# Rows of 276 instead of 272 values for the split activations of a two-block transformer kernel

## What is computed

```python
mod = silu(c) @ ada_w + ada_b            # six shifts, scales and gates
h = modulate(rmsnorm(x, norm1_g), shift1, scale1)
proj = h @ w_in                          # queries, keys, values of two attentions, two gates
merged = sigmoid(ga) * (swa(...) @ w_branch_a) + sigmoid(gb) * (moba(...) @ w_branch_b)
x = x + gate1 * (merged @ w_out)
h2 = modulate(rmsnorm(x, norm2_g), shift2, scale2)
x = x + gate2 * (square(relu(h2 @ w_mlp_in)) @ w_mlp_out)      # 1024 -> 4096 -> 1024
```

```python
h = h + 0.5 * swiglu(rmsnorm(h), w_gate, w_up, w_down)         # 1024 -> 2816 -> 1024
h = h + pool_mixer(...)      or   h + mla_attention(...)       # layer 0, layer 1
h = h + 0.5 * swiglu(...)
```

## Time and profile before

| what | us |
|---|---|
| median of 3 runs | 1241.94 |
| the three runs | 1241.94, 1241.97, 1241.2 |
| span of the profiled execution, first to last instruction | 1239.2 |
| PE busy | 1215.1 (98%) |
| PE weight loads busy | 1192.2 (96%) |
| DVE busy | 862.2 (70%) |
| ACT busy | 634.1 (51%) |
| POOL busy | 174.9 (14%) |

### The profile page before, as it was taken

How to read it: one execution, slowest core, us unless ns; L and a number is a source line. 1 busy time by engine, 2 the same in 40 slices (tenths; PEclk the granted TensorE clock), 3 DMA queues, 4 the chain that set the end, 5 groups by cost and what they waited for, 6 DMA issues and landing times.

```text
span 1239.2 us, 23766 instructions
## 1 busy us (share of the span) xinstructions
PE 1215.1 (98%) x9956; PEld 1192.2 (96%) x9956; DVE 862.2 (70%) x1214; ACT 634.1 (51%) x985; POOL 174.9 (14%) x178
## 2 busy tenths in 40 slices
PE   6999999999999999999999999999999999999997
PEld 4999999999999999999999999999999988999996
DVE  6789888776656766556766665767666777766653
ACT  6557546674445444434544454445454567554531
POOL 3025333000322000012100001310001221000021
PEclk9999999999999999999999999999999999999999
DMA  9987774667564555654455555455555533655641
GB/s 356 326 338 263 245 255 165 233 247 246 166 217 151 181 171 172 202 175 132 134 173 173 180 192 185 148 184 184 199 176 186 188 119 107 205 182 191 198 140 35
DMA packets 67563, 239.17 MB, mean 193 GB/s; under 512 B 7380, under 2 KB 9573, under 8 KB 67456
## 3 DMA queue, kind: packets, MB, share of 16 engines
q1 hardware_dynamic: 66800, 235.41, 56.5%
q0 software_dynamic: 656, 2.24, 0.5%
HBM read 236.55 MB, written 1.07 MB: 192 GB/s over the span
## 4 chain that ended last, share of the span: by engine, by line
PE 93%; DVE 2%; issue 0%; ACT 0%; POOL 0%
PE G L610 28%; PE G L609 28%; PE G L611 28%; PE A L609 1%; PE A L611 1%; PE A L610 1%; DVE sb_wlo L1567 0%; PE A L761 0%; PE A L1055 0%; PE A L776 0%; PE A L749 0%; PE G L1110 0%; PE G L1112 0%; PE G L1111 0%; PE A L1089 0%; PE A L639 0%
## 5 line engine op out<-in xcount | busy, mean ns | idle before, releaser
L1567 DVE TENSOR_TENSOR sb_wlo<-sb_raw,sb_whi 128x1024 fp32r<-128x1024 f32 (+1 forms) x398 | 488.1, 1259 | 81.0 <-ACT sb_whi L1168 80.7
L609 PE MATMUL G<-sb_xh,sb_whi 128*128 128x256 f32 (+2 forms) x1752 | 496.4, 283 | 0.4 <-DVE sb_wlo L1567 0.4
L1168 ACT ACTIVATE sb_whi<-sb_raw 128x1024 fp32r<-128x1024 f32 (+1 forms) x397 | 404.6, 1044 | 180.1 <-PE G L611 161.4
L610 PE MATMUL G<-sb_xl,sb_whi 128*128 128x256 f32 (+2 forms) x1752 | 496.7, 283 | 0.0
L611 PE MATMUL G<-sb_xh,sb_wlo 128*128 128x256 f32 (+2 forms) x1752 | 495.1, 283 | 0.0
L609 PEld LDWEIGHTS G<-sb_xh,sb_whi 128*128 128x128 f32 x1752 | 329.7, 188 | 0.9 <-DVE sb_wlo L1567 0.7
L611 PEld LDWEIGHTS G<-sb_xh,sb_wlo 128*128 128x128 f32 x1752 | 329.4, 188 | 0.0
L610 PEld LDWEIGHTS G<-sb_xl,sb_whi 128*128 128x128 f32 x1752 | 329.2, 188 | 0.0
L609 PE MATMUL G<-sb_hh,sb_whi 128*128 128x256 f32 (+1 forms) x1056 | 297.4, 282 | 1.3 <-DVE sb_hh L1808 1.3
L611 PE MATMUL G<-sb_hh,sb_wlo 128*128 128x256 f32 (+1 forms) x1056 | 297.8, 282 | 0.0
L610 PE MATMUL G<-sb_hl,sb_whi 128*128 128x256 f32 (+1 forms) x992 | 280.8, 283 | 0.0
(11 more groups left out here) (335 smaller groups left out, 1226.7 us busy)
## 6 DMA issues: line engine op xcount, KB each, us to landing
sb_raw<-in_wstream SPq DMA_DIRECT2D x438, 512.0 KB, 4.4
sb_raw<-in_wstream SPq DMA_DIRECT2D x8, 320.0 KB, 7.2
sb_bias<-bias_scratch POOLq DMA_DIRECT2D x1, 2048.0 KB, 16.9
sb_X<-in_xT SPq DMA_DIRECT2D x2, 512.0 KB, 5.2
out_T<-sb_X SPq DMA_DIRECT2D x4, 256.0 KB, 2.7
sb_con<-in_consts SPq DMA_DIRECT2D x1, 601.0 KB, 9.8
sb_band<-in_bands SPq DMA_DIRECT2D x1, 314.0 KB, 5.3
sb_vec<-in_vecs SPq DMA_DIRECT2D x1, 82.5 KB, 2.0
```

What stands on the lines that cost most here:

```text
L609: e.matmul(out, w_h, xs, start=k0 + s.kt == 0, stop=False)
L610: e.matmul(out, w_h, xr, start=False, stop=False)
L1168: e.activation(whi[:, i % NSPLIT, 0:w], raw[:, c % NRAW, 0:w], ACT.Copy).then_inc(hi_done, 1)
L1567: e.tensor_tensor(wlo[:, i % NSPLIT, 0:w], raw[:, c % NRAW, 0:w], f(whi[:, i % NSPLIT, 0:w]), ALU.subtract).then_inc(lo_done, 1)
```

## The change

The rows of `xh` and `xl` become 276 values long, of which the last four are never written or read, and a tile of 32 float32 values per partition, which nothing uses, is put between the two. Two whole-row accesses name their 272 columns instead of `:`. Everything else is as before.

```diff
+XROW = T + 4
...
-        xh, xl = sb("xh", [P, KT, T], F32R), sb("xl", [P, KT, T], F32R)
+        xh = sb("xh", [P, KT, XROW], F32R)
+        sb("pad", [P, 32])
+        xl = sb("xl", [P, KT, XROW], F32R)
...
-                e.activation(xh[:, kt, :], X[:, kt, :], ACT.Identity, scale=V("ffn2_norm0", kt)).then_inc(xh_done, 1)
+                e.activation(xh[:, kt, 0:T], X[:, kt, :], ACT.Identity, scale=V("ffn2_norm0", kt)).then_inc(xh_done, 1)
...
-                e.scalar_tensor_tensor(xl[:, kt, :], X[:, kt, :], V("ffn2_norm0", kt), f(xh[:, kt, :]), ALU.mult, ALU.subtract).then_inc(xl_done, 1)
+                e.scalar_tensor_tensor(xl[:, kt, 0:T], X[:, kt, :], V("ffn2_norm0", kt), f(xh[:, kt, 0:T]), ALU.mult, ALU.subtract).then_inc(xl_done, 1)
```

## The result

The changed kernel takes 1245.03 us (median of 7 runs, 1244.38 to 1245.72) against 1241.66 us for the kernel before (7 runs, 1240.53 to 1241.97): 1.0029 times as long, with a 95% interval of 1.0018 to 1.0040. That is slower by 0.29%; the medians are 3.4 us apart. The time lies inside the range of 1223 to 1246.5, but on the other side of no change.

What follows compares the result with a forecast made beforehand. PE's step between matmuls times their number was taken as the bound. Gains of 4.4 us (256 wide) and 1.6 us (272 and 258 wide) made 6.0 us off 1241.9, forecasting 1235.9 us, range 1223 to 1246.5.

Steps and rivals of the forecast that it cites:

- What bounds the kernel: Whole kernel: PE's step from one matmul to the next times their number sets the pace, not weight splitting or DMA.
- I cost them at nothing: ACT's 272-wide `xh` writes (513 ns) and VectorE's `xl` writes (818 ns): same contiguous values, so no cost.
- The `hh` products at 0: Products reading `hh` and `hl` keep their place against the weights, so their change was taken as 0.
- those 1.7 us: `mlp_out`: an end of the range in which the fast stretch of 127 triples is lost, 1.7 us more.
- Value taken: x matmuls: half way to the fast pace at 256 wide, 4.4 us; an eighth at 272 and 258, 1.6 us; 6.0 less.
- slower, by starts off the grid: Every x product: 1.5 ns on 3366 matmuls starting off the 64-byte grid, 5.0 us, giving 1246.9 us; slower had chance 0.22.
- Its mark in the profile: x steps: 118 ns or more on rows with kt not a multiple of 4, the old figure on kt 0 and 4.
- The price taken for it from the 258-wide rows: 258-wide x matmuls, starting at 56 bytes: 2.5 ns more than 256 wide, 1.0 for two values, 1.5 ns left.
- Nothing happens: x products: 1.84 ns per 16-byte piece of a moving row, pieces unchanged, so 1241.9 us; no change had chance 0.34.
- The 109.2 ns: 256-column matmul: N/2.4 + 2.5 ns by the skill page, wherever columns lie; the trace's 113.3 and 117.7 show it isn't the whole price.

Runs made afterwards that it cites:

- the map: Three kernels, against the kernel before: hidden rows of three MLPs each moved to one constant place behind the weight block; 1243.29, 1245.17 and 1243.57 us, each timed once.

## Why the prediction was wrong

**What bounds the kernel** held: PE's step times the count. All of the difference lies in it, clock and counts equal.

**"I cost them at nothing"**, for ACT's and VectorE's writes at the new pitch, held: VectorE is busy 862.1 us against 862.2, ACT 633.9 against 634.1. **The `hh` products at 0** held: 115.57 and 117.78 ns as before, the 127 fast triples kept. That those 1.7 us could be lost was a real end of the range: five of the experiments' profiles lost them, two of them (the first two of the map) with `mlp_out` and all ahead of it untouched. So that they were kept is in part luck: the addresses don't fix it.

**"Value taken"** is the step that failed. It put the 256-wide x matmuls half way to the fast pace (1.8 ns less, 4.4 us) and the others an eighth of the way (1.6 us), for 6.0 us less. Measured: 1.1 ns *more* at 256 wide, 3.0 us over its three stages; 0.5 ns more at 272 wide, 1.0 us; 0.1 us at 258 wide. The reason given was that starts spread over 8 places pass more of them, the good and the bad. Passing more places brings a gain only if the share of good ones rises, and it fell: one good place is known, 192, it went from two rows in eight to one, and the fast triples in `ffn1_1` and `ffn2_1` from 80 to 40. The trace of before had this in it. The fast triple of the earlier trace rows is a row at place 192; a mean by place over the whole stage would have shown 115.2 against 117.4 to 117.9, and the addresses of the diff show how many rows will stand there. With only before's figures, one row of eight at 115.2 and the rest at 117.6 makes 117.3, 0.3 ns more; the other 0.8 ns comes from the seven other rows, whose mean is 118.4 instead of 117.6, and a little from 192 itself (115.8). Those prices no row of before could tell.

**Rival "slower, by starts off the grid"** gave 1246.9 us and came nearest in sign and size (1.5 ns on 3366 matmuls; measured 0.5 and 1.1). Its mechanism fell: with everything 32 bytes off the grid the x step stayed at 116.96. Its mark in the profile, rows kt 0 and 4 at the old figure, did not come: kt 0 and 4 stood at 64 before and took 117.5; now kt 0 stands at 192 and takes 115.8, kt 4 at 0 and takes 118.7, and kt 7, off the grid, takes 117.4. The price taken for it from the 258-wide rows was not a price of the grid either: they kept 119.5 ns when everything moved by 32 bytes.

**"Nothing happens"**, one figure per 16-byte piece, fell: the pieces are the same in number and the step isn't. The Trainium skill's page "SBUF — State Buffer", section "Door 1: The DMA port swizzle", has lines of 16 bytes and nothing coarser for a reader to pay for; the map of places (113.3 to 120.0 ns at one count of pieces) speaks against carrying that over to PE's reads. Its section "Who interferes with whom" has PE wait for nobody; nothing here shows another engine in it, but a moving row's place against PE's own weights moves the step by up to 6%. The 109.2 ns that the prediction took from the Trainium skill's page "TensorE: Matmul & The Clock Gate", section "Back-to-back issue gap", are given there for an isolated matmul, not for a stream with weight loads; no term of the sum rested on them.

**Not settled.** Why 192 is the good place, what keeps a pace once it is there, and how a row's neighbours enter its step, no run shows. That the moving read and the load of the next weights get in each other's way would fit a figure that depends on their distance alone, but it is an argument; a stream without weight loads was not tried. Nor do the runs say what decides at the break of `mlp_out` whether its second half goes fast: of the three kernels of the map, equal up to there, one kept the fast stretch and two lost it. It is worth 1.7 us, half of what the change cost, so a difference of that size in a single execution of this kernel says nothing of an edit.

## What to carry to other kernels

Where PE streams back to back with a weight load for each matmul, tabulate the step by the moving row's start minus the weight block's start, modulo 256 bytes, before touching a pitch: a mean over a stage hides that one place in the table carries the gain. Then count from the addresses how many rows the edit will put at each place; for the change of this document that count gives the sign. It isn't enough in general: with all eight rows at 192 `ffn1_1` went at 117.8 ns, slower than before's 117.0. A fast pace has to be entered as well as allowed, so read the timeline behind each break, and try a short run of rows at other places ahead of the good one.

## What was not expected of the hardware

- The step of a float32r matmul of 256 columns depends on the distance of two tiles modulo 256 bytes: in streams at one place 113.3 ns at 192 (or 117.8, see below) and 117.8 to 120.0 elsewhere; at 272 columns 123.4 at 192 and 126.7 at 64 and 128. Moving both tiles together by 32 bytes changes nothing, and when the weights alone moved by 128 the fast triples went over to the rows that then stood at 192.
- The same instruction on the same tiles at one place has two lasting paces, 113.3 and 117.8 ns (places 64 and 192), which hold for hundreds of matmuls and across stages, and switch at a break, or behind rows at 64 and 128 (one row at 128 was not enough). At the break of `mlp_out` the switch came in one of three kernels that are equal up to there.
